# Turning attention weights by a float32 product with a diagonal of reciprocal sums

## What is computed

```
s = q k^T / 8 (+ the window's mask)
p = softmax([sink, s])[..., 1:]        # weights over the keys, the sink left out
o = p v
```

## Time and profile before

| | before |
|---|---|
| median of 3 runs | 1406.79 us |
| the profiled execution | 1407.59 us |
| its span in the profile | 1405.8 us |
| PE busy | 1297.4 us (92%) |
| DVE busy | 813.4 us (58%) |
| ACT busy | 685.8 us (49%) |
| mean granted clock of PE | 0.965 |

### The profile page before, as it was taken

The page is one execution under the profiler, slowest core; times in us unless marked ns, Lnnn a source line. Parts: engine busy times, 40 slices in busy tenths (PEclk is TensorE's granted clock), DMA queues, the critical chain, the costliest instruction groups (busy, mean ns, idle before and its releaser), DMA issues.

```text
span 1405.8 us, 19610 instructions
## 1 busy us (share of the span) xinstructions
PE 1297.4 (92%) x7072; PEld 1018.2 (72%) x7072; DVE 813.4 (58%) x1183; ACT 685.8 (49%) x977; POOL 123.9 (9%) x88
## 2 busy tenths in 40 slices
PE   4999978679999999999999976788999999999996
PEld 1678745458688888888877964377888888888875
DVE  2222496853523332333335477666988988898895
ACT  5422343552622311322325354355877877787773
POOL 2200000002011100111120000011000000000080
PEclk9999979799999999999999997899999999999998
DMA  9752237006132321323212434637999999999993
GB/s 368 259 193 99 89 121 270 1 1 266 64 102 98 124 81 60 105 90 118 102 58 83 149 121 152 224 120 272 381 357 373 393 367 354 399 372 359 370 400 130
DMA packets 96719, 282.78 MB, mean 201 GB/s; under 512 B 8704, under 2 KB 10256, under 8 KB 96400
## 3 DMA queue, kind: packets, MB, share of 16 engines
q1 hardware_dynamic: 90880, 264.27, 51.8%
q0 software_dynamic: 3472, 12.06, 2.3%
q10 hardware_dynamic: 2304, 5.58, 1.0%
HBM read 270.86 MB, written 11.01 MB: 201 GB/s over the span
## 4 chain that ended last, share of the span: by engine, by line
PE 81%; DVE 8%; ACT 4%; DMA 3%; issue 2%; SPq 0%; ACTq 0%; DVEq 0%
PE ps L734 14%; PE ps L736 13%; PE ps L735 13%; PE ps L1158 6%; PE ps L1159 5%; PE ps L1160 5%; PE ps L1175 3%; PE ps L1177 3%; PE ps L1173 3%; PE ps L711 3%; DMA raw<-in_w_mod 2%; PE ps L827 2%; PE ps L829 2%; PE ps L828 2%; PE ps L997 1%
## 5 line engine op out<-in xcount | busy, mean ns | idle before, releaser
L622 DVE TENSOR_TENSOR wlo<-raw,whi 128x1024 fp32r<-128x1024 f32 (+2 forms) x271 | 353.5, 1320 | 273.4 <-ACT whi L617 271.9
L617 ACT ACTIVATE whi<-raw 128x1024 fp32r<-128x1024 f32 (+2 forms) x271 | 298.2, 1107 | 211.2 <-PE ps L736 138.8
L734 PE MATMUL ps<-hhi,whi 128*128 128x512 f32 (+1 forms) x736 | 276.6, 376 | 5.9 <-DVE hlo L1800 4.2
L735 PE MATMUL ps<-hlo,whi 128*128 128x512 f32 (+1 forms) x736 | 273.1, 371 | 0.0
L736 PE MATMUL ps<-hhi,wlo 128*128 128x512 f32 (+1 forms) x736 | 273.0, 371 | 0.0
L734 PEld LDWEIGHTS ps<-hhi,whi 128*128 128x128 f32 x736 | 138.8, 189 | 43.0 <-issue 11.9
L736 PEld LDWEIGHTS ps<-hhi,wlo 128*128 128x128 f32 x736 | 139.0, 189 | 26.8
L735 PEld LDWEIGHTS ps<-hlo,whi 128*128 128x128 f32 x736 | 139.1, 189 | 25.8
L622 DVE TENSOR_TENSOR xlo<-raw,xhi 128x1024 fp32r<-128x1024 f32 (+1 forms) x98 | 134.0, 1374 | 28.3 <-ACT xhi L617 27.5
L617 ACT ACTIVATE xhi<-raw 128x1024 fp32r<-128x1024 f32 (+1 forms) x98 | 114.3, 1168 | 36.5 <-PE ps L1177 18.6
L1158 PE MATMUL ps<-whi,hs_hi 128*128 128x512 f32 (+1 forms) x256 | 95.4, 373 | 1.1 <-DVE hs_lo L2156 0.7
(11 more groups left out here) (318 smaller groups left out, 2094.7 us busy)
## 6 DMA issues: line engine op xcount, KB each, us to landing
raw<-in_w_gu SPq DMA_DIRECT2D x230, 512.0 KB, 5.8
raw<-in_w_dn SPq DMA_DIRECT2D x80, 704.0 KB, 8.7
raw<-in_w_mod SPq DMA_DIRECT2D x52, 512.0 KB, 5.0
raw<-in_w_fm SPq DMA_DIRECT2D x32, 512.0 KB, 3.6
mraw<-in_w_mod SPq DMA_DIRECT2D x24, 512.0 KB, 6.2
raw<-in_w_out SPq DMA_DIRECT2D x16, 512.0 KB, 4.6
y_rows<-zrow POOLq DMA_DIRECT2D x1, 4608.0 KB, 18.8
raw<-in_w_tg SPq DMA_DIRECT2D x8, 512.0 KB, 3.5
```

The costliest lines, as they stand in the source:

```text
L617: nc.scalar.activation(high(v)[:, 0:cols], src[:, 0:cols], ACT.Copy).then_inc(hi_ready, 1)
L622: nc.vector.tensor_tensor(low(v)[:, 0:cols], landed_in(v)[0][:, 0:cols], high(v)[:, 0:cols].bitcast(F32), ALU.subtract).then_inc(lo_ready, 1)
L734: nc.tensor.matmul(outp, whs, xh, start=first, stop=False)
L735: nc.tensor.matmul(outp, whs, xl, start=False, stop=False)
```

## The change

The weights in `prob` stay as the exponential left them. DVE no longer multiplies them. It multiplies the identity matrix by the reciprocal sums instead, which gives a 128x128 diagonal matrix `rdiag` for each head, in two buffers of its own. PE turns each block of weights by an ordinary float32 product with `prob` stationary and `rdiag` moving, which turns and scales at once. The normalising of a step waits additionally, from the third step on, for the turn that last read the same buffer of `rdiag`. Everything else stands in the same order on every engine, and the number of products in a turn is the number of transposes before.

```diff
@@ -215,6 +215,7 @@
         prob = sb("prob", [P, 2, 2, T], F32, region)
         probT = sb("probT", [P, 2, 2, T], F32, region)
+        rdiag = sb("rdiag", [P, 2, 2, P], F32, region)
@@ -994,8 +995,9 @@
                         for k in range(keys(todo[i][0])):
-                            mm = nc.tensor.transpose(ps[:, 4 + kv, k * P:(k + 1) * P],
-                                                     prob[:, i % 2, kv, k * P:(k + 1) * P], ident[:, :])
+                            mm = nc.tensor.matmul(ps[:, 4 + kv, k * P:(k + 1) * P],
+                                                  prob[:, i % 2, kv, k * P:(k + 1) * P], rdiag[:, i % 2, kv, :],
+                                                  start=True, stop=True)
                         mm.then_inc(pT_done[l], 1)
@@ -2054,7 +2056,9 @@
                         for kv, ready in ((0, pn_ready[l]), (1, pn2_ready)):
-                            V.tensor_scalar(prob[:, (i - 1) % 2, kv, 0:n], prob[:, (i - 1) % 2, kv, 0:n],
+                            if i >= 3:
+                                dve.wait_ge(pT_done[l], 2 * (i - 3) + kv + 1)
+                            V.tensor_scalar(rdiag[:, (i - 1) % 2, kv, :], ident[:, :],
                                             rden[:, c - 2 + kv:c - 1 + kv], None, ALU.mult
                                             ).then_inc(ready, 1)
```

## The result

The changed kernel took 1408.61 us, the median of 20 runs, against 1402.74 for 20 runs of the kernel before: ratio 1.0048, 95% interval 1.0033 to 1.0062, or 4.6 to 8.7 us slower, +6.7 in the middle; the medians differ by 5.9. The forecast was +5.8.

What follows compares the result with a forecast made beforehand. TensorE carries the chain of waits nearly everywhere; in attention's steady steps a two-step loop between engines was the bound. Longer turns +6.6 us and clock -0.8 gave +5.8 on 1406.79, so 1412.6 us, range 1407.5 to 1417.5, 8 in 10.

Steps and rivals of the forecast that it cites:

- A: Attention loop of one step: exponentials, copy of turned weights, next turn; from 3.39 to 4.23 us, becoming the bound.
- B: Attention loop of two steps: exponentials, turn, weights times values, scores, DVE's maximum; from 7.36 to 8.10 us, bound before.
- The turn's price: Eight products in place of eight transposes: 0.74 us more to TensorE's next start, 0.84 more to their end.
- The loops' sum: Longer turns in attention at 2.4 GHz: +1.9 and +1.5 in layer 0, +1.9 and +1.3 in layer 1, +6.6 us.
- The clock: Four attention stretches at 1.2 GHz: first and third held at full clock, others fallen; -0.8 us, bounds -4.5 and +3.8.
- DVE's saving: Scaling on DVE in attention: 7.6 us less busy time, hidden, so taken as 0, bounds 0 and -0.4.
- the added wait: Scaling's wait for an earlier turn in attention: already met when DVE arrives, so 0.
- Loop C: Where a query tile ends: exponentials, copies, tails on ACT and DVE, next maximum; 4.56 us, no turn, unchanged.
- the first: Rival: denser turns keep 2.4 GHz in all four low-clock attention stretches; +2.1 us, 1408.9, chance 0.18.
- second: Rival: the clock falls in all four attention stretches as before; +10.4 us, 1417.2, chance 0.18.
- third: Rival: TensorE alone is the bound in attention, every turn shows whole; 16.4 us and more, 1423, chance 0.04.
- fourth: Rival: DVE's queue sets the pace in attention, its 7.6 us come off the path; faster, 1399, chance 0.04.

Runs made afterwards that it cites:

- half the products: Kernel before, with the first head's blocks turned by float32 products with the identity, the second head's by transposes: 1405.74 us, ratio 1.0022.
- the control: The kernel before, unchanged, run and profiled again: 1402.59 us, ratio 1.0002.
- the product alone: Kernel before, with blocks turned by float32 products with the identity instead of transposes, DVE still scaling the weights in place: 1411.52 us, ratio 1.0059.
- the diagonal alone: Changed kernel, with transposes of the unscaled weights in place of products, normalisation left out of the result: 1794.53 us, with the experts' work doubled.
- the first run of products in the first turn: Kernel before, with only each layer's first turn made by float32 products with the identity: 1399.36 us, ratio 0.9971; repeated, 1403.35 us, 0.9997.
- the one-pass kernel: Changed kernel, with `prob` and `rdiag` in fp32r, a reduced float32 format, so each product is one pass: 1410.77 us, ratio 1.0050.

## Why the prediction was right, and where it was not

The time lies in the range, and sign and mechanism came out as forecast; two terms of the sum did not. The time itself, 1408.61, is 4.0 us under the 1412.6 forecast and 1.1 above the range's lower end, because the three runs that the sum started from (1406.79) lie 4.1 above the median of 20 (1402.74); the difference is what the sum can be judged by.

- *A takes over from B.* Right: 4.29 us a step against 4.23 forecast, released by the turn. With half the products the two loops' sums, 3.85 for A and 7.82 for two steps of B, were met to 0.02 us.
- *The turn's price* was too low. I took the difference to the next start, 1.78 - 1.04 = 0.74, for loop B and for TensorE, and 0.84 to the end for A. A turn of eight lasts 2.02 us in the changed kernel, not 1.95, against 1.11 before: 0.91 to its end; to the next start it is 1.95 (267.62 to 269.57) against 1.04, again 0.91. My 1.78 came from a row where passes and the next series follow each other every 0.11 us; in a turn the second pass starts 0.18 us after the first, and the next products 0.21 us after the last. The transposes' 1.04 had such pauses in it, the 1.78 had not.
- *The loops' sum* at full clock, +6.6 forecast: by the marks of the two traces +2.12 in layer 0's steady steps (1.9), +1.83 in those after them (1.5), and in layer 1 +2.13 (1.9) and +1.53 (1.3): 7.6. The turn's price makes some 0.6 of the 1.0 us: 0.06 in each of six steady steps, about as much in two whole turns after them, and 0.45 instead of 0.36 for four products in the step over 256 keys where A holds. Most of the rest is two shares that I had estimated: the two steps over 256 keys with slack took 0.47 together and not 0.3, and the turn before the last in layer 1 took 0.58 and not 0.42.
- *The clock*, -0.8 forecast from two stretches held and two fallen: all four held, and the four places gave -1.43, -0.37, -0.30 and -0.80, together -2.9. Each is smaller than the end that I gave it for a clock that holds (-2.0, -0.9, -0.5, -1.1). In part the longer turns in them were priced too low as well; in part a clock that holds gives back less than I took, because the exponentials behind then wait for the longer turn, loop A: in layer 1 the step from 5.57 us (910.14 to 915.71 before) fell to 4.29, 1.28 saved where I had 1.7. 7.6 - 2.9 is the 4.7 us of the pair of traces. The two errors have opposite signs, +1.0 in the loops and -2.1 in the clock, and they depend on the pair: against the control the change costs 6.9 in the same stretches, which leaves some 0.7 for the clock. That +5.8 came so near the runs (+5.9 by the medians, +6.7 by the ratio) is in part luck.
- *Why the clock held* I had put to the longer turn ahead of each fall. One longer turn did not do it. With longer turns in every step the clock was at 2.4 GHz from the fourth exponentials of each layer on, in the profiles of the changed kernel, the product alone and the doubled transposes; ahead of those the doubled transposes still had a fall, at 265.1 us. Over the runs the mean clock rose from 0.966 (34 runs) to 0.971 (20), in 1404 us some 13 us less at 1.2 GHz. But the unchanged kernel's falls in attention differ between its own executions, and two profiles with turns of the old length in the steady steps (the diagonal alone, and the first run of products in the first turn) have no fall after the first steps either, from about 268 us on. So how much of the -2.9 is the change's doing stays open.
- *The Trainium skill's* remark that transpose mode doesn't bring up the full clock ("TensorE: Matmul & The Clock Gate", section Part 4: PE-mode transpose) is not what these runs show: with doubled float32 transposes in every step, beside the scores and the products with the values, the clock was 1.00 from 268.6 on. Nor is its factor of four for FP32 (section Terms): 16 passes take 0.91 us more than eight transposes, 1.82 times to the ends.
- *DVE's saving and the added wait at 0*: right, shown by each half alone. *Loop C*: right, 4.56. *Nothing outside attention changes*: the traced pair differs there by 2.0 and 2.3 us, the control by 2.4 and 1.3, so nothing contradicts it.
- The rivals: in the profile the clock held everywhere, as the first said, but its price of +2.1 was too low (+4.7 in the traced pair), by the same turn and by what a held clock gives back. The second, third and fourth did not occur.

## What to carry to other kernels

When an operation gets longer inside a pipeline of engines, write down every loop that passes through it with its period and how often it is passed; the new period is the largest of the new sums, and the cost isn't the length times the count. The loops tell what to reorder as well: taking one stage out of the loop that set the pace and splitting one wait gave 0.5%, where a scaling moved off an engine with slack gave nothing. And take a duration to the next start from a place with the same neighbours.

## What the runs showed of the hardware

A one-pass fp32r product over 128 columns takes the same time in a series as a float32 transpose (turns of eight at full clock: 1.11 us both, at 275.10 in the one-pass kernel), and the granted clock is lower with it: 0.77 and 0.71 in the one-pass kernel's stretches against 0.87 to 0.94 in the two profiles of the kernel before, and 0.954 against 0.966 in the mean of the runs. A product with half the passes lost 0.5% of the whole kernel against transposes that way. What in these passes makes the difference no run here isolates.
